# More products of ones around the norm sums of a kernel of two transformer stacks

## Time and profile before

| | before |
|---|---|
| median of 3 runs | 2414.69 us (2409.95 to 2415.71) |
| the profiled execution: its own time | 2414.04 us |
| its span, first to last instruction | 2412.3 us |
| TensorE busy | 96% of the span |
| VectorE, ScalarE busy | 70%, 42% |
| chain that ended last, by engine | PE 79%, DVE 13%, ACT 5%, issue 2% |
| mean granted clock of TensorE | 0.989 of full |
| records of products of ones (L733) | 206, of 103 products |

### The profile page before, as it was taken

One profiled execution on the slowest core, in us unless ns is written; L12 is line 12 of the kernel. 1 busy time (PEld: TensorE's weight loads), 2 busy tenths in 40 slices (PEclk: granted clock), 3 DMA queues, 4 the chain that ended last, 5 costly groups with the idle time before them and its releaser, 6 DMA issues.

```text
span 2412.3 us, 31291 instructions
## 1 busy us (share of the span) xinstructions
PE 2316.7 (96%) x12282; PEld 1940.6 (80%) x12282; DVE 1684.1 (70%) x2754; ACT 1016.8 (42%) x1593; POOL 31.5 (1%) x65
## 2 busy tenths in 40 slices
PE   7999999999999999999899999899999999988998
PEld 4888878877787888887788999666788888867998
DVE  6876567456588886777778778687675555776655
ACT  4422222256634322224655545565431332466543
POOL 0000000010000000000000000000000000000000
PEclk9999999999999999999999999999999999999999
DMA  8355435442442454343314564212245344323553
GB/s 346 125 208 202 175 140 203 184 171 105 149 165 101 144 183 175 137 142 122 127 53 140 184 195 160 70 53 79 98 163 206 129 182 175 100 71 115 183 187 128
DMA packets 99132, 360.33 MB, mean 149 GB/s; under 512 B 11096, under 2 KB 14552, under 8 KB 96808
## 3 DMA queue, kind: packets, MB, share of 16 engines
q1 hardware_dynamic: 94600, 341.46, 40.3%
q0 software_dynamic: 4384, 16.86, 2.0%
HBM read 350.94 MB, written 5.24 MB: 148 GB/s over the span
## 4 chain that ended last, share of the span: by engine, by line
PE 79%; DVE 13%; ACT 5%; issue 2%; DMA 1%; SPq 0%; DVEq 0%; ACTq 0%
PE PS L673 63%; PE PS L873 3%; DVE w_lo L1968 3%; PE PS L701 3%; PE PS L1089 2%; ACT w_hi L1312 1%; PE PS L915 1%; PE PS L889 1%; DVE conv L2781 1%; PE PS L1282 1%; ACT probs L1823 1%; PE PS L1211 1%; DVE xv L2406 1%; DVE h_lo L2396 1%; PE PS L1019 1%
## 5 line engine op out<-in xcount | busy, mean ns | idle before, releaser
L1968 DVE TENSOR_TENSOR w_lo<-raw,w_hi 128x1024 fp32r<-128x1024 f32 (+1 forms) x456 | 543.2, 1209 | 290.2 <-ACT w_hi L1312 288.7
L1312 ACT ACTIVATE w_hi<-raw 128x1024 fp32r<-128x1024 f32 (+1 forms) x456 | 460.5, 1041 | 459.5 <-PE PS L673 444.5
L673 PE MATMUL PS<-h_hi,w_hi 128*128 128x512 f32 (+1 forms) x1456 | 475.1, 334 | 4.3 <-DVE h_lo L2396 2.8
L673 PE MATMUL PS<-h_hi,w_lo 128*128 128x512 f32 (+1 forms) x1400 | 469.5, 335 | 0.0
L673 PE MATMUL PS<-h_lo,w_hi 128*128 128x512 f32 (+1 forms) x1336 | 451.3, 338 | 0.0
L673 PEld LDWEIGHTS PS<-h_hi,w_hi 128*128 128x128 f32 x1456 | 270.4, 188 | 33.6 <-issue 2.7
L673 PE MATMUL PS<-hid_hi,w_hi 128*128 128x512 f32 (+1 forms) x864 | 290.0, 336 | 2.1 <-DVE w_lo L1968 2.1
L673 PE MATMUL PS<-hid_hi,w_lo 128*128 128x512 f32 (+1 forms) x864 | 288.7, 334 | 0.0
L673 PE MATMUL PS<-hid_lo,w_hi 128*128 128x512 f32 (+1 forms) x864 | 288.6, 334 | 0.0
L673 PEld LDWEIGHTS PS<-h_hi,w_lo 128*128 128x128 f32 x1400 | 264.1, 189 | 27.7
L673 PEld LDWEIGHTS PS<-h_lo,w_hi 128*128 128x128 f32 x1336 | 252.0, 189 | 27.4 <-issue 0.2
(11 more groups left out here) (441 smaller groups left out, 3767.3 us busy)
## 6 DMA issues: line engine op xcount, KB each, us to landing
raw<-in_weights SPq DMA_DIRECT2D x434, 512.0 KB, 4.5
ada_ring<-in_ada SPq DMA_DIRECT2D x176, 512.0 KB, 3.7
raw<-in_weights SPq DMA_DIRECT2D x22, 384.0 KB, 4.1
og<-in_ada SPq DMA_DIRECT2D x4, 1024.0 KB, 11.8
qk<-in_ada SPq DMA_DIRECT2D x4, 1024.0 KB, 16.8
m_hi<-h_spill POOLq DMA_DIRECT2D x4, 1024.0 KB, 8.2
wgt<-in_x SPq DMA_DIRECT2D x4, 512.0 KB, 17.6
h_spill<-h_hi POOLq DMA_DIRECT2D x1, 2048.0 KB, 8.4
```

Source lines behind the costliest of these rows:

```text
L673: mm = pe.matmul(out, a, b, start=(k == 0 and i == 0), stop=(k == ph.k_tiles - 1 and i == 2))
L1312: act.activation(w_hi[:, s, 0:w], raw[:, s, 0:w], ACT.Copy).then_inc(sem("w_hi"), 1)
L1968: dve.tensor_tensor(w_lo[:, s, 0:w], raw[:, s, 0:w], w_hi[:, s, 0:w].bitcast(F32), ALU.subtract)\
```

## The change

In the RMS places (the branch without `mean`) 22 products of ones are added ahead of the wait for the sum where the tile is full, and 12 where it is not. Behind the sums, in the places that had products there, their number rises from 14 to 30 (full) and 8 to 24 in the layer-norm places, and from 14 to 28 (full) and 7 to 22 in the RMS places. Nothing else changes. This is the whole diff:

```diff
                 else:
                     linear(name, hi, lo, **more)
+                    keep_busy(22 if full else 12)
                     pe.wait_ge(sem("var"), ncall[0])
                     ncall[0] += 1
                     nsq[0] += 8
                     pe.wait_ge(sem("sq_used"), nsq[0])
                     pe.matmul(PS[:, 5, r], ones[:], RSTD[:, r], start=True, stop=True).then_inc(sem("xsum"), 1)
                 if name not in ("g1out1", "f1out1"):
-                    keep_busy(({True: 14, False: 8} if mean else {True: 14, False: 7})[full])
+                    keep_busy(({True: 30, False: 24} if mean else {True: 28, False: 22})[full])
```

## The result

The changed kernel takes 2420.24 us (median of 9 runs, 2418.59 to 2421.16) against 2415.24 us for the kernel before, run beside it (9 runs, 2409.95 to 2417.80): a ratio of 1.0021, with an interval of 1.0012 to 1.0029. It is 5.0 us slower, clear of no change, and within the 0.3% named ahead. The forecast was 2418.6 us, 4.6 us above the profiled execution of before.

The account below looks back on a forecast made before the run. TensorE, busy 96% of the span, bounds the kernel; added products hide only in its waits. Terms 0.2 + 0 + 0 + 3.1 + 0.7 + 0.1 + 0.5 = 4.6 us on 2414.04 give 2418.6 us; range 2415 to 2422, with rivals 2412.0 to 2425.0.

Parts of the forecast that it names:

- The price of a product: On TensorE, two records of 0.112 us each, 0.224 us per product; 159 added products make 35.6 us.
- wo0: RMS place: sum 1.53 us late, then 28 products set the front's start with no wait to absorb it; +3.1 us.
- g0out1: RMS place: front 1.9 us late, part taken up by a wait inside the front; +0.7 us.
- wo1: RMS place: front 1.76 us late, but the clock staying up gives back 1.6; +0.1 us.
- g1out1: RMS place at the end of the chain: sum late behind the products ahead of it; +0.5 us.
- mout and f0out1: Layer-norm places: front's waits for h_lo take up the late products; +0.2 us at mout, 0 at f0out1.
- (b): Rival, 13%: lateness is never made up, each place passes on its whole overrun; 9.1 us in all, 2423.1 us.
- aout: Layer-norm place: products end 1.16 us later, but the splitting of weights limits what follows; 0.
- (c): Rival, 5%: the clock falls although products run, at wo0, g0out1 and wo1; 10.7 us, 2424.7 us.
- (d): Rival, 7%: products fit, sums coming later in most runs or products costing half in idle waits; 2411.5 us.
- (a): Rival, 15%: slow stretches stood elsewhere in timed runs, so wo1 and g0out1 give nothing back; 7.1 us, 2421.1 us.
- credits of the clock: Time given back by a clock that stays up: 1.6 us at wo1, 0.9 at g0out1's sum; without them 7.1.

Follow-up runs that it names:

- mean_undone: Against the changed kernel: the three layer-norm places go back to 14, 14 and 8 products, RMS places stay; 2419.88 us, ratio 1.0021.
- wo0_undone: Against the changed kernel: only place wo0 goes back to no product ahead of the sum and 14 behind; 2417.80 us, ratio 1.0014.
- ahead_only: Against the changed kernel: products ahead of the sums stay (22 and 12), counts behind them as in the kernel before; 2413.97 us, ratio 0.9996.
- fitted: Against the changed kernel: counts cut to fit the waits, 14 and 9 ahead of the sums, 15 to 24 behind; 2412.11 us, ratio 0.9993.
- behind_only: Against the changed kernel: no products ahead of the sums, only those behind (30, 24, 28, 22); 2417.62 us, ratio 1.0013.
- aout_only: Against the kernel before: 24 products instead of 8 behind place aout alone; 2415.82 us, ratio 1.0000.
- fitted_again: The kernel fitted, unchanged, run a second time in the second group; 2412.23 us, ratio 0.9988 to the kernel before.
- none: Against the changed kernel: no products of ones at any norm; 2417.63 us, ratio 1.0017.

## Why the prediction was right, step by step

**The price of a product** held: 44 records end 4.91 us behind the end of the record before them, 0.1116 us each, at wo0, g0out1 and (24 in 2.68) at wo1 and g1out1. Everything that was sized by it held too: the sum of wo0 1.52 us late (forecast 1.53), that of wo1 2.80 - 2.34 = 0.46 (0.48).

**mout and f0out1** went as said. At mout the front began 1.0 us later and no wait was left in it; the place lost 0.13. At f0out1 the front's third step still stands behind a wait for `h_lo` of 0.88 us, where it was 0.99, and nothing is passed on. mean_undone agrees, over twelve runs: the layer-norm places together cost far less than the 3.4 us of (b).

**wo0** was the largest term, and wo0_undone shows it: -2.4 us by the medians for a term of 2.91 by the places. The mechanism was that said ahead: the sum late behind 22 products, then 28 products longer than the work between the sum and `h`, and a front with no wait that could absorb it. The forecast was 0.2 too high, as the sum took 1704.85 - 1703.99 = 0.86 us and not 0.94, and the 28 products 1711.02 - 1704.85 = 6.17 and not 6.27.

**g0out1, wo1 and g1out1** came within 0.1 us each. At g0out1 the front began 1.70 us late (forecast 1.9), and its matmul that had stood behind a wait for `h_lo` at 2074.51 came 0.79 late without one (forecast 0.77). The split of weights behind the front took nothing more off: the wait for `w_lo` is 1.24 us in after and was 1.25 in before, so 0.70 is passed on.

```profile
2078.53 0.50 PE L673 MATMUL PS<-h_hi,w_hi 128*128 128x512 f32 x1 [1.25 <-DVE w_lo L1968]
```

At wo1 the price of the products and the gain of the clock cancel. That gain was 1.5 us, and it belongs to the products ahead: ahead_only and fitted have it (18.07 us), behind_only does not (20.85 us). It was no luck of one profile of before: in all four profiles with no product ahead of the sum the clock fell there.

**aout** is the step that failed, by half a microsecond. It was taken as 0 because the splitting of weights hides everything up to 1361 us. That holds for lateness of TensorE's products: behind_only has 24 of them and takes 88.75 us, 0.06 more than before. It does not hold for the sums, which VectorE reads. The first sum and VectorE in before, and VectorE in after:

```profile
1271.50 0.70 PE L789 MATMUL PS<-xv,ones 128*128 128x256 f32 x2 [1.36 <-DVE xv L2319]
...
1273.04 2.35 DVE L1968 TENSOR_TENSOR w_lo<-raw,w_hi 128x1024 fp32r<-128x1024 f32 x2
1275.31 0.42 DVE L2429 SCALAR_TENSOR_TENSOR xv<-PS,xv 128x256 f32<-128x256 f32 x1
...
1276.73 0.42 DVE L2430 SCALAR_TENSOR_TENSOR xv<-PS,xv 128x256 f32<-128x256 f32 x1 [0.49 <-PE PS L797]
```

In before VectorE's splits of weights (L1968) ended later than the sums, and its first step that reads the last sum (L2429) began 1275.31 - 1271.50 = 3.81 us behind the first sum. In after the sums ran at the low clock from L793 on (1.19 us for its two records, 0.67 in before), VectorE stood idle for the last one (L797), and the step began 1276.73 - 1272.35 = 4.38 us behind the first: 0.57 late. That is the whole 0.57 of the place, and the splits behind it pass it on. The other profiles agree: where the clock fell as early as in after (aout_only, fitted_again) the step came 0.57 and 0.58 late and the place took 0.55 and 0.56 more; where it fell one record later (wo0_undone) both are 0.30; where it fell two records later (behind_only) the place lost 0.06; where it stayed up (fitted, mean_undone, none, ahead_only) nothing. So the forecast's cover, the split, ends about where the sums end at the full clock, and the bounds looked only at the products.

Why the clock fell in the sums is open. The rows before had shown no low clock there. It was found in all four profiles with 24 products, in one of two with 18, and in none of the four with 8 or none. Products can't slow what runs ahead of them, and fitted and fitted_again show both clocks for one program, so I leave open whether this is more than chance.

**The rivals.** (b) fell with mean_undone. (c) did not happen in the changed kernel at its three places, where the clock was 1.00, but its mechanism exists: at wo1 of behind_only, with the wait ahead of the sum open, the clock fell while products ran, as it had at wo0 in before. (d) is answered by the traces: two records per product at 0.112 each, in the idle wait as well. (a) happened in part, and elsewhere than I put it: both credits of the clock, at wo1 and in g0out1's sum, came as counted, and most of the 1.8 us of the span that no place explains are slow stretches in work that the change does not touch.

**How close the number came** is in part luck. The places give 4.8 us for a forecast of 4.6, with aout 0.57 too low and wo0 0.2 too high. The medians give 5.0, while single profiles of this kernel differ by some 3 us in work that no edit touches.

**The Trainium skill**, TensorE: Matmul & The Clock Gate, Part 1, says that the number of slow matmuls at a kernel's start varies between runs of one kernel, and that one should not fit to it. In mid-kernel the runs agree with it for stretches that no product covers: 0.79 and 1.00 at the same stretch of one program (fitted and fitted_again, 360 to 372 us). For the credits of this change the sum with them (4.6) came nearer to the 4.8 of the places than the one without (7.1).

## What to carry to other kernels

Work put into a wait to keep an engine busy must be counted against that wait with its measured price: here the kernel gained or kept its time while the work ended inside the wait (fitted), and lost time once it ended behind the wait on a path without slack (wo0). Of idle time that is gone from a trace, ask first what now stands in its place: here 18.6 us of waits vanished and the kernel lost 5 us. And before you call a stretch covered by another engine, look at everything that engine reads: at aout VectorE was covered against late products and not against late sums. An overrun costs only where nothing behind it waits anyway, so cut the fill first at the places whose front has no wait left, and leave the others.

## What the runs showed of the hardware that I had not expected

- **The clock of one program differs between executions far ahead of any edit.** All these kernels have the same instructions up to the sum of mout, and reach it at 739.75 us (fitted_again, ahead_only), 741.4 (before, after) or 743.1 (fitted, mean_undone). From 348 to 372 us the granted clock accounts for it: in fitted it was 0.92 for 12 us and 0.79 for 12, 0.96 + 2.52 = 3.5 us lost, against 743.12 - 739.75 = 3.37 measured. So two single profiles of this kernel can differ by some 3 us as a whole. A place compares to within 0.1 us where the clock was the same in both, and to 0.6 or 0.7 where it was not (aout in fitted and fitted_again, mout in before and ahead_only).
- **The same idle wait was followed by a fall of the clock in one kernel and not in the other.** Behind 3.25 us at wo0 the clock was 1.00 in behind_only and 0.50 in before; behind 14 products and an idle 2.3 us at mout it was 0.86 from 744 to 756 us in ahead_only and aout_only, and 1.00 in before and mean_undone; the place took 0.7 us longer in the first two. With 24 or 30 products there it was 1.00 in every profile (five).
- **At wo1 the clock went with the idle time ahead of the sum, not with the products behind it.** In the six profiles with 9 or 12 products ahead the clock was 1.00 from 2220 to 2232 us, with 7 to 22 behind; in the four with none ahead (before, none, aout_only, behind_only) it was 0.82 to 0.87, with 0 to 22 behind. 22 products behind took 5.07 us in the one case and 6.70 in the other.
